# Samples' attention in a hybrid decoder step: four sequences at a time in 32-column strips, other load order and issuers

## The reference, cut to what matters

```
o_c, p_c = compressed_attention(q, q_pos, kcc, vcc)      # 63 compressed keys a sequence
idx      = select_blocks(p_c, q_pos, kb.shape[2])        # 16 of 17 blocks of 64 keys
o_s      = selected_attention(q, q_pos, idx, kb, vb)     # keys and values of the 8 pages, and new ones
o_w      = window_attention(q, q_pos, k_all, v_all, ...) # 512 window rows, and new ones
o_attn   = gates[..., 0:1] * o_c + gates[..., 1:2] * o_s + gates[..., 2:3] * o_w
x = x + concat(rmsnorm(o_attn), rmsnorm(o_conv)) @ w_out
```

## Time and profile before

| | us |
|---|---|
| runs | 3343.47, 3346.35, 3346.39; median 3346.35 |
| span of the profiled execution | 3342.5 |
| PE busy | 3222.5 (96%) |
| VectorE busy | 1657.1 (50%) |
| ScalarE busy | 368.8 |
| GpSimd busy | 50.8 |
| samples' attention, from the prompt's last values to the third product of the output projection | 968.7 to 1154.86 |

### The profile page before, as it was taken

The page is one execution under the profiler, slowest core; times in us unless marked ns, Lnnn a source line. Parts: engine busy times, 40 slices in busy tenths (PEclk is TensorE's granted clock), DMA queues, the critical chain, the costliest instruction groups (busy, mean ns, idle before and its releaser), DMA issues.

```text
span 3342.5 us, 41158 instructions
## 1 busy us (share of the span) xinstructions
PE 3222.5 (96%) x14592; PEld 2591.0 (78%) x14592; DVE 1657.1 (50%) x3410; ACT 368.8 (11%) x898; POOL 50.8 (2%) x79
## 2 busy tenths in 40 slices
PE   8999999899878999999999999999999999999998
PEld 7788877788545788577888888888888888888876
DVE  7798232353633334313644544554455445456456
ACT  3000020111532000212100000000000000000013
POOL 0000000100000000000000000000000000000002
PEclk9999999999978999999999999999999999999999
DMA  6222223340024621462322322232223223213222
GB/s 223 63 67 71 66 77 114 108 129 17 1 102 141 202 76 62 145 210 75 101 77 65 107 78 77 67 107 76 67 77 107 75 63 100 88 50 108 82 55 92
DMA packets 309664, 306.92 MB, mean 92 GB/s; under 512 B 12664, under 2 KB 295932, under 8 KB 307759
## 3 DMA queue, kind: packets, MB, share of 16 engines
q1 hardware_dynamic: 297978, 278.81, 26.6%
q0 software_dynamic: 2928, 18.69, 1.6%
q10 hardware_dynamic: 8640, 7.87, 0.8%
HBM read 291.36 MB, written 23.14 MB: 94 GB/s over the span
## 4 chain that ended last, share of the span: by engine, by line
PE 77%; DVE 2%; ACT 1%; DMA 1%; issue 1%; ACTq 0%; SPq 0%; DVEq 0%
PE ps L950 57%; PE ps L1276 5%; PE ps L914 3%; PE ps L1600 2%; PE ps L919 2%; PE ps L1466 2%; PE ps L1315 1%; PE ps L1427 1%; PE ps L1395 1%; PE ps L1303 0%; PE ps L1304 0%; ACT xT_region_b L1884 0%; PE ps L1378 0%; PE ps L1579 0%; PE ps L1245 0%
## 5 line engine op out<-in xcount | busy, mean ns | idle before, releaser
L950 PE MATMUL ps<-xT_region_b,weight_ring 128*128 128x272 f32 x2080 | 491.0, 392 | 1.1 <-DVE weight_ring L2142 1.1
L950 PEld LDWEIGHTS ps<-xT_region_b,weight_ring 128*128 128x128 f32 x2080 | 395.3, 190 | 82.7 <-issue 1.5
L950 PE MATMUL ps<-region_c,weight_ring 128*128 128x272 f32 x1664 | 401.3, 393 | 1.0 <-DMA weight_ring<-in_w_out 1.0
L950 PEld LDWEIGHTS ps<-region_c,weight_ring 128*128 128x128 f32 x1664 | 315.8, 190 | 66.3 <-DMA weight_ring<-in_w_out 1.2
L919 PE MATMUL ps<-xT_region_b,weight_ring 128*128 128x272 f32 x1536 | 354.6, 394 | 2.7 <-DVE region_c L2110 1.1
L919 PEld LDWEIGHTS ps<-xT_region_b,weight_ring 128*128 128x128 f32 x1536 | 292.2, 191 | 63.7 <-issue 3.9
L950 PE MATMUL ps<-region_f 128*128 128x272 f32 x1408 | 336.9, 392 | 0.0
L950 PEld LDWEIGHTS ps<-region_f 128*128 128x128 f32 x1408 | 267.6, 190 | 55.0
L950 PE MATMUL ps<-region_f,weight_ring 128*128 128x272 f32 x960 | 229.9, 393 | 0.0
L1714 ACT ACTIVATE ext<-ps 128x272 f32<-128x272 f32 x100 | 39.7, 397 | 1647.9 <-PE ps L950 1636.1
L950 PEld LDWEIGHTS ps<-region_f,weight_ring 128*128 128x128 f32 x960 | 182.4, 190 | 37.6 <-issue 0.2
(11 more groups left out here) (390 smaller groups left out, 3731.1 us busy)
## 6 DMA issues: line engine op xcount, KB each, us to landing
weight_ring<-in_w_ffn_gate SPq DMA_DIRECT2D x44, 1024.0 KB, 5.0
weight_ring<-in_w_ffn_up SPq DMA_DIRECT2D x44, 1024.0 KB, 5.0
weight_ring<-in_w_in SPq DMA_DIRECT2D x36, 1024.0 KB, 5.2
weight_ring<-in_w_ffn_down SPq DMA_DIRECT2D x64, 512.0 KB, 4.1
weight_ring<-in_w_out SPq DMA_DIRECT2D x16, 1024.0 KB, 5.2
weight_ring<-in_w_ffn_down SPq DMA_DIRECT2D x32, 384.0 KB, 3.7
region_f<-in_cache_k_cmp SPq DMA_DIRECT2D x64, 128.0 KB, 2.1
region_f<-in_cache_v_cmp SPq DMA_DIRECT2D x64, 128.0 KB, 2.0
```

The source lines that it names most:

```text
L950: mm = pe.matmul(prod(k, r), lhs[:, t, :], rhs[:, t, :], start=(t == 0), stop=(t == m - 1))
```

## The change

- Rows of the samples are numbered anew: partitions 32 s to 32 s + 31 hold sequences s and 4 + s (16 rows each). `QP` shrinks to 32 columns a sequence and kv head.
- Scores: keys come in 12 chunks. A chunk is one group of four sequences (`which`), one kv head and half of the pages (chunks 0 to 7) or the window (8 to 11); four banks of turns, then four products of 512 columns, each from its own 32 weight columns into its own 32 partitions. Turned keys have three buffers. Each chunk is turned before the scores of the one before it.
- The pages come first and the window last, so the page softmax lies among the chunks 7 to 11, and only the window softmax follows the scores. The window rows are read four in a row for each partition (4 KB).
- Values: `strips` makes for four sequences in turn the same piece (page or window part), into four strips; the groups of four sequences follow each other as page values 0, window values 0, page values 1, window values 1. The number of products stays 240, the turns' number stays too.
- Loads: SP issues the key pages of sequences 0 to 3 before it waits for prompt attention's end (after the `cmp` jobs); GpSimd issues the key and value pages of sequences 2, 3 (values) and 6, 7 (both), from `s_pv` 6 on; ScalarE issues none. Four and more buffers hold whole groups.
- The residual comes back in two halves, after the third and the fourth values group (`s_so` 3 and 4), not after prompt attention.

The diff, cut to its core (helpers of the copies on ScalarE mirror those of VectorE):

```diff
-    b, t = q // 16, q % 4
+    b, t = 4 * (q // 16 % 2) + q // 32, q % 4
...
-                        ("s_cmp", 4), ("s_win", 2 * NB), ("s_sel", 4 * NB), ("s_p", 8), ("s_o", 4),
+                        ("s_ka", 16), ("s_cmp", 4), ("s_kb", 32), ("s_p", 8), ("s_o", 4),
...
-        QP = flat(RB, 256, KV, NB, P)
+        QP = flat(RB, 256, KV, NB, 32)
...
+        TKEY = [flat(RF, 2304, 2048), flat(RB, 4608, 2048), flat(RB, 6656, 2048)]
+        LATE = T_KC * TOK
+        KRAW = [[flat(XR, 4352, 2048), flat(XR, 6400, 2048), ring(4608, 2048), flat(RC, LATE, 2048)],
+                [ring(0, 2048), ring(2048, 2048), flat(XR, 0, 2048), flat(XR, 2048, 2048)]]
+        WRAW = [[flat(VTF, 0, 4, KVW), flat(VTF, 1024, 4, KVW), flat(RC, LATE, 4, KVW), flat(RC, LATE + 1024, 4, KVW)],
+                [flat(XR, 4352 + 1024 * s, 4, KVW) for s in range(4)]]
+        VSEL = [KRAW[1], [ring(4608, 2048), flat(VTF, 0, 2048), flat(XR, 4352, 2048), flat(XR, 6400, 2048)]]
+        VWIN = [[flat(RC, LATE, 4, KVW), flat(RC, LATE + 1024, 4, KVW), flat(RF, 2304, 4, KVW), flat(RF, 3328, 4, KVW)],
+                [flat(XR, 1024 * s, 4, KVW) for s in range(4)]]
...
+        def pages(eng, name, slots, which, h, seqs, landed):
+            for s in seqs:
+                for k in range(4 * h, 4 * h + 4):
+                    at = (4 * which + s) * PAGES + k
+                    page = eng.value_load(PTB[0:1, at:at + 1], min_val=0, max_val=79)
+                    eng.dma_start(slots[which][s][:, k * KVW:(k + 1) * KVW],
+                                  A[name][0, ds(page, 1)].rearrange("o t k d -> (o t) (k d)")).then_inc(landed, 16)
+
+        def window_rows(eng, name, slots, which, seqs):
+            for s in seqs:
+                eng.dma_start(slots[which][s], A[name][0, 4 * which + s].rearrange("(p t) k d -> p t (k d)", t=4)).then_inc(s_swn[which], 16)
...
+            sp.wait_ge(s_tr, end_of("cmp"))
+            for h in range(2):
+                pages(sp, "cache_k_sel", KRAW, 0, h, range(4), s_spg[0][h])
+            for h in range(2):
+                pages(sp, "cache_k_sel", KRAW, 1, h, (0, 1), s_spg[1][h])
+            window_rows(sp, "cache_k_win", WRAW, 0, (0, 1))
+            sp.wait_ge(s_tr, key_at(3, 3) + 1)
+            window_rows(sp, "cache_k_win", WRAW, 0, (2, 3))
+            window_rows(sp, "cache_k_win", WRAW, 1, range(4))
+            for h in range(2):
+                sp.wait_ge(s_tr, key_at(5 + 2 * h, 3) + 1)
+                pages(sp, "cache_v_sel", VSEL, 0, h, (0, 1), s_spg[0][h])
+            sp.wait_ge(s_kt, 10)
+            window_rows(sp, "cache_v_win", VWIN, 0, range(4))
+            for h in range(2):
+                pages(sp, "cache_v_sel", VSEL, 1, h, (0, 1), s_spg[1][h])
...
-            sp.wait_ge(s_so, NB - 1)
-            load_out(0, 0, slice(0, 256))
-            sp.wait_ge(s_so, NB)
-            load_out(0, 1, slice(0, 256))
+            sp.wait_ge(s_so, 1)
+            window_rows(sp, "cache_v_win", VWIN, 1, range(4))
+            for j in range(2):
+                load_out(0, j, slice(0, 256))
+            sp.wait_ge(s_so, 3)
             for j in range(2):
...
+            def turn_keys(c):
+                which, kv, h = key_chunk(c)
+                if kv == 0:
+                    if h is None:
+                        pe.wait_ge(s_swn[which], 64)
+                    else:
+                        pe.wait_ge(s_spg[which][h], 128 if which else 256)
+                        if which:
+                            pe.wait_ge(s_ppg[h], 128)
+                for s in range(4):
+                    k = key_at(c, s)
+                    tr_bank(k)
+                    for a in range(4):
+                        ins = turn(bank(k)[:, a * P:(a + 1) * P], key_rows(c, s, a))
+                    ins.then_inc(s_tr, 1)
+
+            def key_scores(c):
+                which, kv, h = key_chunk(c)
+                if c == 8:
+                    pe.wait_ge(s_imr, 2)
+                turned(pe, key_at(c, 3) + 1)
+                for s in range(4):
+                    mm = pe.matmul(PS[32 * s:32 * s + 32, 4 + kv if h is None else 2 * kv + h, :], QP[:, kv, 4 * which + s, :],
+                                   TKEY[c % 3][:, 512 * s:512 * (s + 1)], start=(which == 0), stop=(which == 1))
+                mm.then_inc(s_kt, 1)
+
+            turn_keys(0)
...
+            for c in range(1, 4):
+                turn_keys(c)
+                key_scores(c - 1)
...
+            for c in range(6, 12):
+                turn_keys(c)
+                key_scores(c - 1)
+            key_scores(11)
...
+            def strips(u, kv, probs, values, start=False, stop=False):
+                for s in range(4):
+                    mm = pe.matmul(PS[32 * s:32 * s + 32, 2 * u + kv, 0:DH], probs[:, 32 * s:32 * s + 32], values(s), start=start, stop=stop)
+                return mm
+
+            def page_values(u):
+                for h in range(2):
+                    pe.wait_ge(s_spg[u][h], 256 if u else 384)
+                    pe.wait_ge(s_ppg[2 if u else h], 256)
+                    for a in range(4 * h, 4 * h + 4):
+                        for kv in range(KV):
+                            at = a * KVW + kv * DH
+                            mm = strips(u, kv, PTS[:, kv, a, :], lambda s: VSEL[u][s][:, at:at + DH])
+                mm.then_inc(s_so, 1)
+
...
+            for u in range(2):
+                for kv in range(KV):
+                    strips(u, kv, PCG[0:NC_S, kv, :], lambda s: VC[0:NC_S, (4 * u + s) * KV + kv, :], start=True)
+            turned(pe, jobs["s_p"] + 5)
+            for u in range(2):
+                for kv in range(KV):
+                    strips(u, kv, PTS[0:SAMP, kv, 8, :], lambda s: VT[0:SAMP, 4, kv, :])
+            page_values(0)
+            pe.wait_ge(s_ss_, 4)
...
+            window_values(0)
+            page_values(1)
+            rows_turned(0)
+            window_values(1)
...
+            keys_copied(7)
+            dve.wait_ge(s_imr, 2)
+            dve.wait_ge(s_kt, 7)
+            page_largest(0)
+            keys_copied(8)
+            dve.wait_ge(s_kt, 8)
+            page_largest(1)
+            keys_copied(9)
+            page_scaled(0)
+            keys_copied(10)
+            page_scaled(1)
+            keys_copied(11)
...
+            rows_copied(0)
...
-            dve.wait_ge(s_xb, 16)
+            dve.wait_ge(s_xb, 32)
...
-            pool.wait_ge(s_pv, 8)
+            pool.wait_ge(s_ptb, 16)
             pool.wait_ge(s_sp, 16)
-            pool.dma_start(XR[:, 0:KT * TOK], SPILL).then_inc(s_xb, 16)
+            pool.wait_ge(s_pv, 6)
+            for h in range(2):
+                pages(pool, "cache_k_sel", KRAW, 1, h, (2, 3), s_ppg[h])
+            for h in range(2):
+                pool.wait_ge(s_tr, key_at(5 + 2 * h, 3) + 1)
+                pages(pool, "cache_v_sel", VSEL, 0, h, (2, 3), s_ppg[h])
+            pool.wait_ge(s_tr, key_at(11, 3) + 1)
+            for h in range(2):
+                pages(pool, "cache_v_sel", VSEL, 1, h, (2, 3), s_ppg[2])
+            MID = KT * TOK // 2
+            pool.wait_ge(s_so, 3)
+            pool.dma_start(XR[:, MID:KT * TOK], SPILL[:, MID:KT * TOK]).then_inc(s_xb, 16)
+            pool.wait_ge(s_so, 4)
+            pool.dma_start(XR[:, 0:MID], SPILL[:, 0:MID]).then_inc(s_xb, 16)
```

More of the change, by code:

```diff
@@ L1337, in _ @@
+            turn_keys(0)
             pe.wait_ge(s_q, 1)
             pe.wait_ge(s_scr, 32)
+            pe.wait_ge(s_ccr, 8)
             pe.wait_ge(s_ov, 8)
             for kv in range(KV):
[L1341 to L1344 removed]
@@ L1380, in _ @@
[L1380 to L1397 removed]
+                    turn(bank(k)[:, 0:P], SOUT[:, quarter, kv, :]).then_inc(s_tr, 1)
@@ new lines, in window_values @@
+            def window_values(u):
+                pe.wait_ge(s_swn[u], 128)
+                for a in range(4):
+                    for kv in range(KV):
+                        mm = strips(u, kv, PTS[:, kv, 9 + a, :], lambda s: VWIN[u][s][:, a, kv * DH:(kv + 1) * DH], stop=(a == 3))
+                mm.then_inc(s_so, 1)
+            for kv in range(KV):
+                pe.wait_ge(s_ss_, 2 + kv)
+                for m in range(2):
+                    k = jobs["s_p"] + 2 * kv + m
+                    tr_bank(k)
+                    for a in range(4):
+                        ins = turn(bank(k)[:, a * P:(a + 1) * P], PSS[:, kv, (4 * m + a) * P:(4 * m + a + 1) * P])
+                    ins.then_inc(s_tr, 1)
@@ new lines, in _ @@
+            page_values(0)
+            pe.wait_ge(s_ss_, 4)
+            for kv in range(KV):
+                k = jobs["s_p"] + 5 + kv
+                tr_bank(k)
+                for a in range(4):
+                    ins = turn(bank(k)[:, a * P:(a + 1) * P], PSW[:, kv, a * P:(a + 1) * P])
+                ins.then_inc(s_tr, 1)
+            k = jobs["s_p"] + 7
+            tr_bank(k)
+            for kv in range(KV):
+                ins = turn(bank(k)[0:SAMP, kv * P:(kv + 1) * P], PSW[:, kv, WIN:WIN + SAMP])
@@ L1937, in _ @@
```

(2 more changed lines are left out.)

387 lines of the change are left out of this document (158 added, 229 removed).

## The result

| | before | after |
|---|---|---|
| median of the runs | 3345.73 us | 3250.62 us |
| lowest to highest | 3343.47 to 3346.39 | 3249.63 to 3253.03 |
| profiled execution's own time | not on record | 3249.63 |
| its span | 3342.5 | 3248.0 |

A forecast was written before the change was run, and what follows sets the result against it. TensorE, 96% busy, was taken as the bound. Walk 81.0 us, tail 14.5 and allowance 8 gave a stage of 103.5 against 186.2, saving 82.7: 3264 us, range 3250 to 3280, to 3300 with rivals (a), (c), (e).

The forecast's parts named there:

- Strips: Scores and values: four matmuls in different strips run together, 12.0 us against 41.2 for scores, 16.8 against 58 for values.
- Rival (b): Scores and values: strips take turns, one after the other, +60 us, time 3324; chance 0.04.
- (d): Scores and values: every change of strip drains the array, +112 us, slower than before at 3376; chance 0.02.
- Opening and half clock: Stage start: 7.0 us for placing queries, chunk 0 and first scores, plus 1.5 for half clock in the first chunks.
- Rival (c): Whole stage: VectorE's copies, softmaxes and norm in one order are the bound, +18 us, time 3282; chance 0.15.
- GpSimd's pages: Page loads: 1.15 us an issue, last 16 issued at 1038 and landed at 1041, making PE wait 3.7 us.
- rival (e): Page loads: GpSimd issues a page in 2.5 us, +16 us, time 3280; chance 0.09.
- the walk: Stage from 968.7 us: PE's pieces added in order, 81.0 us to the values' end at 1049.7 instead of 1141.8.
- The allowance of 8 us: Whole stage: 8 us added to 95.5 for hand-overs and uneven landings the walk leaves out, giving 103.5.
- Tail: After the values' end, to the output projection's third product: 14.5 us, being VectorE 5.8 us late plus 8.7.
- Rival (a), transfers: Whole stage: 21 MB at 190 GB/s take 110 us and bound it, time 3285; chance 0.15.
- The residual's return at nothing: After the values: return in two halves lands near 1068, costed at nothing; 4 to 8 us without PE's cover.

The follow-up runs named there:

- the kernel with half pages: Against the changed kernel, only rows 0 to 63 of each of the second half's 32 value pages were fetched, with as many issues: 3257.67 us.
- the last kernel: Against the changed kernel, norm taken earlier, three second-half value pages issued before the first window rows, two pages moved from GpSimd to SP: 3258.16 us median.
- Three attempts to shorten it: Against the changed kernel: second-half value pages issued earlier, 3258.24 us; that plus an earlier norm, 3260.02; earlier norm with a small shift of pages, 3258.16.
- the early norm: Against the changed kernel, squares' product moved to chunk 8's scores, root behind chunk 10's copies, reciprocal behind chunk 11's: 3251.21 us.

## Why the prediction was right, step by step

The mechanism was right and the forecast 13 us too high. The stage lasts 1062.31 - 970.6 = 91.7 us, predicted 103.5, before 186.2; that is 94.5 of the 95.1. It starts 1.9 us later than before, and what follows it is 1.9 us shorter.

- **Strips.** Scores: predicted 1.0 us a group, measured 1.00. Values: predicted 0.28, measured 0.23 in the page values; the hand-overs of 0.03 taken from the memory attention don't show at 128 columns. Scores in one strip cost 29.6 us, values in turn 26 of PE time. Rival (b), strips in turn, and (d), a drain at each, fall with that. On the rule of the Trainium skill (TensorEngine Tiling (Array Packing), Key Properties) that only a change of tiling mode drains: the group of 1.00 us is two records of 0.43 and 0.14 over, which leaves room for one change of form and none for a drain at each strip.
- **Opening and half clock.** 7.0 and 1.5 predicted, 4.9 and 0 measured. The experiment with chunk 0 behind the first scores shows that the turns there keep the clock at 2.4 GHz. I had assumed half clock in the first chunks in any case. I had also put the half clock before down to the softmax; it began earlier, behind PE's wait of 3.3 us for the placed queries:

```profile
972.07 3.68 PE L1343 MATMUL ps<-region_c,xT_region_b 128*128 128x63 f32 x16 [3.34 <-DVE xT_region_b L2558]
```

- **Key chunks with scores and VectorE's work between.** 45.7 predicted (with the importance products and the 1.5 of half clock), 1019.44 - 975.43 = 44.0 measured. Rival (c) is out: PE's waits for copies in the stage are all of 0.6 us or less.
- **Turns of the page probabilities.** 3.4 predicted, 3.1 measured.
- **GpSimd's pages.** 1.15 us each was exact but for two of them (1.45), and rival (e) is out. The wait for them was predicted 3.7 and is 8.3: PE arrived at 1034.15, 3 us earlier than in the walk, and the last page landed 1.3 us later than there, since it took 6.0 us to land and not 3. The Trainium skill's rule (SBUF — State Buffer, SBUF: two separate sides) that VectorE's two-port copies keep GpSimd from writing descriptors doesn't show: the distance of issues stayed 1.15 us beside the reciprocal and the products. VectorE's copies there read PSUM. One scaling within SBUF (0.77 us from 1011.72, row above) lay beside two issues, and the distance was 1.15 us there too; what a plain copy within SBUF would do no run here shows.
- **Values' end.** The walk gave 81.0 us, measured 1050.55 - 970.6 = 80.0. That it comes so near is partly luck: opening -2.1, key chunks -1.7, turns -0.3, and from the first value to the last +3.1 (28.0 against 16.8 + 2.8 + 5.3), which is the longer wait for pages.
- **The allowance of 8 us** is the step that failed. I had added it "for hand-overs and uneven landings" on top of a walk whose distances were already measured from operation to operation, waits of 0.3 us in them, and which had 5.0 for VectorE besides. PE's small waits for copies and scalings in the stage sum to 7.6 us (rows below), and they lay inside the terms.
- **Tail.** 14.5 predicted, 11.8 measured, and both of its parts were off. I had VectorE 5.8 us late; its last sum is done at 1050.3 and its copy of the last rows starts at 1050.69, so it is not late at all. The reason is PE's longer wait for pages: the values end 20.3 us after the start of the squares' product, not 15. The other part, 8.7, should have been 11.8; I had taken the first product out of it for VectorE's lateness (and 12.9 - 3.7 - 1.0 is 8.2, not 8.7). Behind the last values only the sample squares' norm holds PE back, at the third product (2.2 us).
- **Rival (a), transfers.** Not the bound of the whole stage, but of its last part: share 0.93 in 1023 to 1051 and 1.01 after. As a count of bytes over a mean rate it was the wrong form; by the experiments what bites is the order in which few transfers meet.
- **The residual's return at nothing.** Right for the changed kernel (VectorE waited 2.35 us for it, PE not at all). PE had products to go on with, as predicted. What the prediction didn't see is that an earlier start can hold up the slabs of w_out; by the table above PE's wait for pages kept the start late enough, and that is luck.

The waits of PE between 968 and 1075 us after (us in total, times, longest):

```profile
PE ps L1414 <- DMA xT_region_b<-in_cache_v_sel: 8.3, 1, 8.3
PE ps L920 <- ACT xT_region_b L1748: 3.6, 12, 0.4
PE ps L956 <- DVE region_c L2751: 2.2, 1, 2.2
PE ps L920 <- DVE region_f L2154: 1.5, 3, 0.6
PE ps L920 <- ACT region_f L1748: 1.2, 4, 0.3
PE ps L920 <- DVE xT_region_b L2154: 1.0, 2, 0.6
PE ps L920 <- DVE xT_region_b L2710: 0.3, 1, 0.3
```

8.0 (allowance) + 2.7 (tail) + 1.0 (walk) make the 11.7 us of the stage, to rounding. The other 1.2 us of the 13 are outside it: 0.6 between the stage's saving and the medians', and 0.6 because the kernel before now has a median of 3345.73 and not 3346.35. I had also read 3.9 us around the span; where an execution's own time is on record it is 1.6 to 1.9 us above its span, which changes nothing in the saving.

**Where the 94.5 us came from.** Scores 12 x (3.43 - 1.00) = 29.2. Values: 58 before; after 3.0 (compressed and new, 12 groups) + 3.7 + 5.9 (half clock) + 3.8 (window) = 16.4, so 41.6. PE's idle time in the stage fell from 28.6 to 18.0, 10.6. The other 13 are half clock at the start and work that no longer waits its turn; I don't split them. These are not independent: without the early keys 29.8 us go again (3280.38 us).

**What stays open.** That the transfers started by `s_so` 3 delay the second slab rests on traces that agree, not on a kernel in which they alone were moved. Which of them does it, the residual's return or the third and fourth slab of w_out, these traces can't tell, since both start within 0.3 us of each other; only the landing order in the kernel with half pages points to the residual. Holding either back until the third product, with the pages early, wasn't tried. Why the last kernel has two levels wasn't seen, since no trace of the upper one was taken. Nor was it tried whether the changed kernel's last value page would land sooner if it went out ahead of the window loads.

## What to carry to other kernels

Small products with 32 or fewer output rows belong in different strips in immediate succession: interleaving alone, with no other edit, made them 3.5 times as fast. Once that is done, look at what the faster engine triggers. Here window rows and weights landed just in time behind the one visible wait, and transfers that hang on a semaphore of the values started earlier whenever the wait was shortened, close behind the weights needed first. Three attempts to shorten it lost 7.6 to 9.5 us on the median. A walk made from measured distances already holds the small waits, so an allowance on top counts them twice; here it made most of the miss. A short piece of ready work in front of a wait can be worth more than its own time when it keeps the clock up (4.5 us here for 1.7 us of turns).

## What the runs showed of the hardware

- Two records of an fp32 matmul of 128 columns, in a row of such in one strip, take 0.20 us; four such matmuls in four strips 0.23 together, and at 512 columns 1.00 against 3.43.
- An idle PE pays twice. After the 8.3 us wait the granted clock is 0.50 (1037 to 1043), and 64 matmuls take 5.9 us instead of 3.7. Even after a wait of 2.2 us for VectorE the 16 records of the third product took 3.9 us in one execution of the changed kernel, 5.6 in another and 6.6 with the early norm, which is a scatter of 1.7 to 2.7 us from this one place.
- Fewer bytes made a kernel slower: 2 MB less, 7.1 us more on the median (3257.67).
- An issue on SP's queue can itself be held: one slab's took 0.65 us in the changed kernel and the next one's 4.4, and one in the kernel with half pages 12.6.
- Transfers reached 412 GB/s over 17 us in the kernel with half pages (1043 to 1060). The Trainium skill (SBUF — State Buffer, SBUF: two separate sides) gives about 436 GB/s for the DMA side, which the trace comes near to.
